# Four key tiles instead of five at both ends of a windowed attention, and the first two expert turns prepared one stage earlier

## What is computed

```python
def one_block(b):                       # b: one tile of 128 queries, 8 of them
    q0 = b * Q_BLOCK
    kb = lax.dynamic_slice_in_dim(k_pad, q0, span, axis=1)      # span = 128 + 2 * 128 keys, padded with zeros at both ends
    kpos = q0 + offs
    mask = (jnp.abs(qi[:, None] - offs[None, :]) <= WINDOW) & ((kpos >= 0) & (kpos < L))[None, :]
    return sink_attend(qb, (kb, k_ctx), (vb, v_ctx), (mask, None), sinks)
...
p = softmax(concatenate(parts + [sink], axis=-1))
...
xb = x_pad[rows]                        # experts: the rows of the tokens that chose expert e
hb = jax.nn.silu(xb @ w_gate[e]) * (xb @ w_up[e])
y.at[rows].add((hb @ w_down[e]) * wb[:, None])
```

## Time and profile before

| | |
|---|---|
| median of 3 runs | 2992.59 us |
| lowest and highest run | 2986.41 and 2995.37 us |
| the profiled execution | 2990.77 us, its span 2989.0 us |
| mean granted clock of TensorE | 0.979 of full speed |
| attention, first to last PE instruction | 259.8 to 556.7 us, granted clock 1.00 from 300 us on |
| mixing of layer 0, then its experts | 558.3 to 795.1 us, then from 797.3 us |
| experts of layer 1 | from 2050.4 us |

### The profile page before, as it was taken

How to read it: one execution, slowest core, us unless ns; L and a number is a source line. 1 busy time by engine, 2 the same in 40 slices (tenths; PEclk the granted TensorE clock), 3 DMA queues, 4 the chain that set the end, 5 groups by cost and what they waited for, 6 DMA issues and landing times. The chain is left out here.

```text
span 2989.0 us, 40809 instructions
## 1 busy us (share of the span) xinstructions
PE 2821.1 (94%) x15284; PEld 1368.5 (46%) x15287; DVE 1753.3 (59%) x3359; ACT 509.5 (17%) x1060; POOL 532.5 (18%) x404
## 2 busy tenths in 40 slices
PE   8998999999899999999999598997999999999994
PEld 3444666544444444444444264543444444444442
DVE  4994555466656555555555455665565555555555
ACT  1113555201110111111111240011110111111112
POOL 0000000111022222222222211101222222222212
PEclk9999999999999999999999899998999999999997
DMA  9777200201599999999999622017999999998996
GB/s 365 258 271 215 78 15 8 77 29 42 206 338 331 310 299 321 328 339 329 353 306 321 208 99 83 29 50 282 306 296 332 296 366 320 320 345 275 311 325 197
DMA packets 147086, 715.70 MB, mean 239 GB/s; under 512 B 16702, under 2 KB 21950, under 8 KB 94665
## 3 DMA queue, kind: packets, MB, share of 16 engines
q1 hardware_dynamic: 104252, 556.83, 48.6%
q0 software_dynamic: 42336, 154.16, 20.8%
q10 hardware_dynamic: 304, 2.11, 0.2%
HBM read 598.18 MB, written 114.84 MB: 239 GB/s over the span
## 5 line engine op out<-in xcount | busy, mean ns | idle before, releaser
L1668 PE MATMUL exG<-ring,xT 128*32 128x512 f32 (+2 forms) x2352 | 683.4, 596 | 5.2 <-DMA ring<-in_exp_w_up_dram 3.7
L1479 DVE COPY xT<-exX 128x512 f32<-128x512 f32 x146 | 101.0, 692 | 680.5 <-PE exX L1656 680.2
L1668 PEld LDWEIGHTS exG<-ring,xT 128*32 128x32 f32 (+2 forms) x2352 | 240.0, 141 | 348.0 <-issue 343.4
L1702 PE MATMUL exD<-ring,ex_hT 128*32 128x512 f32 (+2 forms) x1176 | 353.2, 603 | 1.7 <-DVE w_fnet L1517 0.8
L1612 ACT ACTIVATE ex_hT<-exH 128x256 f32<-128x256 f32 x144 | 55.2, 383 | 1454.5 <-PE exH L1690 1454.5
L1485 DVE RECIPROCAL ex_e<-ex_e 128x256 f32<-128x256 f32 x142 | 249.0, 1753 | 5.0
L1668 PE MATMUL exG<-oT,xT 128*32 128x512 f32 (+2 forms) x592 | 192.5, 597 | 1.3 <-DVE xT L1479 1.3
L1426 POOL DMA_INDIRECT y_scratch<-w_fnet,idx_out x72 | 136.1, 1891 | 299.1 <-DMA y_scratch<-w_fnet,idx_out 156.3
L1426 POOL DMA_INDIRECT y_scratch<-w_o,idx_out x72 | 132.8, 1844 | 306.3 <-DMA y_scratch<-w_o,idx_out 166.8
L1449 DVE TENSOR_TENSOR mod<-place,slots 128x1024 bf16<-128x1024 f32 (+3 forms) x196 | 174.1, 912 | 8.1 <-PEq L235 7.4
L1668 PE MATMUL exG<-w_fnet,xT 128*32 128x512 f32 (+2 forms) x608 | 172.2, 599 | 4.8 <-DMA ring<-in_exp_w_up_dram 4.8
(11 more groups left out here) (414 smaller groups left out, 4338.8 us busy)
## 6 DMA issues: line engine op xcount, KB each, us to landing
ring<-in_exp_w_gate_dram SPq DMA_DIRECT2D x64, 1024.0 KB
ring<-in_exp_w_up_dram SPq DMA_DIRECT2D x64, 1024.0 KB
ring<-in_exp_w_down_dram SPq DMA_DIRECT2D x64, 1024.0 KB
ada_w<-in_w_ada_dram SPq DMA_DIRECT2D x48, 512.0 KB, 5.6
oT<-in_exp_w_gate_dram SPq DMA_DIRECT2D x17, 1024.0 KB, 10.4
oT<-in_exp_w_up_dram SPq DMA_DIRECT2D x17, 1024.0 KB, 14.1
oT<-in_exp_w_down_dram SPq DMA_DIRECT2D x17, 1024.0 KB
fT<-in_exp_w_gate_dram SPq DMA_DIRECT2D x17, 1024.0 KB, 10.4
```

The lines of the kernel that those rows point to most:

```text
L1479: dve.tensor_copy(xT[:, par, 0:KT // 2], psX[:, 0:KT // 2]).then_inc(xT_d, 1)
L1668: last = pe.matmul(psG[par][p:p + m], xT[:, par, k, p:p + m], ring[s % RING][:, 0:2, k * FF:(k + 1) * FF], start=k == 0, stop=k == KT - 1)
L1702: last = pe.matmul(psD[p:p + m, c], hT[:, k * P + p:k * P + p + m], ring[s % RING][:, 2, k * D + c * 512:k * D + (c + 1) * 512], start=k = ...
```

## The change

The first and the last query tile no longer touch the key tile that lies outside the sequence: two near tiles and two context tiles, 512 columns for a head instead of 640. `near_tiles`, `width` and `halves_of` give the tiles, the columns and the two halves of a pair's buffer. The mask is now three 128-column tiles that all query tiles share, and its load comes ahead of the first load of the queries. In a pair of an end tile all context products wait on `near_mm`.

In the mixing stage the first two turns are prepared instead of one: both one-hot matrices, both sets of indices, both gathers; `down(7)` goes ahead of the index products. The split of the routing weights and the reading out of the first two turns' weights move into the experts' stage, the latter (`first_weights`) into the middle of the first `gate_up`. The indices of turn 3 are read out in the middle of the second `gate_up`.

```diff
-    none = np.full((P, P), gone)
-    mask = np.stack([np.stack([none if t == 0 else before, 0 * none, none if t == NT - 1 else after], 1) for t in range(NT)], 1)
+    mask = np.stack([before, 0 * before, after], 1)
...
+                def near_tiles(t):
+
+                    return range(max(0, t - 1), min(NT, t + 2))
+
+                def width(p):
+
+                    near = len(near_tiles(p // PAIRS)) * P
+                    return near, near + CTX
...
+                        sp.dma_start(mask[:].rearrange("p t s -> p (t s)").bitcast(mybir.dt.uint16), A["mask"]).then_inc(mask_in, 16)
                         load(0)
-                        sp.dma_start(mask[:].rearrange("p t s -> p (t s)").bitcast(mybir.dt.uint16), A["mask"]).then_inc(mask_in, 16)
...
+                            if len(tiles) < 3:
+                                pe.wait_ge(near_mm, p + 1)
+                                for j in range(2):
+                                    last = pe.matmul(sc[j][:, W:S], q[j], far[j], start=True, stop=True)
+                                last.then_inc(score_mm, 1)
+                                return
...
-                        pool.wait_ge(idx_done, 1)
-                        pool.indirect_dma_start(out=xg[:, 0], out_offset=None, in_=u_dram,
-                                                in_offset=bass.IndirectOffsetOnAxis(ap=idx[:, 0:1], axis=0)).then_inc(gathered[0], 16)
+                        pool.wait_ge(idx_done, 2)
+                        for b in range(2):
+                            pool.indirect_dma_start(out=xg[:, b], out_offset=None, in_=u_dram,
+                                                    in_offset=bass.IndirectOffsetOnAxis(ap=idx[:, b:b + 1], axis=0)).then_inc(gathered[b], 16)
...
+                        def weight_parts():
+                            link = Links(dve, parts_own)
+                            for c in range(3, 6):
+                                link(dve.tensor_copy(moving[:, :, :, c], w_rest))
+                                if c < 5:
+                                    link(dve.tensor_tensor(w_rest, w_rest, moving[:, :, :, c], ALU.subtract))
+
+                        def first_weights():
+                            dve.wait_ge(first_mm, 1)
+                            dve.tensor_reduce(w_all[:, 0:2], psD[:, :, 3:6], AX, ALU.add).then_inc(first_own, 1)
+                            dve.tensor_copy(idx_all[:, 0:2], idx[:])
...
-                        onehot(1, 1)
-                        indices(0, 0, 2)
+                        rows(0, 0, 2)
+                        weight_parts()
+                        first_weights()
                         onehot(2, 0)
-                        indices(1, 1, 2)
-                        rows(0, 0, 2)
+                        rows(1, 1, 2)
                         indices(2, 0, 2)
-
                         onehot(3, 1)
-                        rows(1, 1, 2)
+                        hidden(0, 0, 2)
                         indices(3, 1, 2)
-                        hidden(0, 0, 2)
...
                             for k in range(KT):
+                                if b == 0 and k == KT - 2:
+                                    first_weights()
+                                if b == 1 and k == KT // 2:
+                                    index(3, 1)
```

More of the change, by code:

```diff
@@ L698, in heads, with halves_of @@
                     return t, (2 * c + a) * 4 + 2 * half
-                def slot(t, j):
-                    return t + j if j < 3 else NT + 2 + j - 3
+                def near_tiles(t):
[3 more added lines that the diff above has]
+                    return near, near + CTX
+                def slot(t, j):
+                    near = near_tiles(t)
+                    return near[j] + 1 if j < len(near) else NT + 2 + j - len(near)
+                def halves_of(p, buf):
+                    s = width(p)[1]
+                    return [buf[:, j * s:(j + 1) * s] for j in range(2)]
                 with nc.Block() as block:
@@ L852, in scores @@
                             at_least(pe, copied_d, p - 1)
-                            sc = pair[p % 2]
+                            sc, tiles, (W, S) = halves_of(p, pair[p % 2]), near_tiles(t), width(p)
                             q = [qT[j * HD:(j + 1) * HD, t % 2, k] for j in range(2)]
-                            near = [kT[j * HD:(j + 1) * HD, kv, t * P:t * P + W] for j in range(2)]
+                            near = [kT[j * HD:(j + 1) * HD, kv, slot(t, 0) * P:slot(t, 0) * P + W] for j in range(2)]
@@ L856, in scores @@
                             far = [kT[j * HD:(j + 1) * HD, kv, (NT + 2) * P:(NT + 2) * P + CTX] for j in range(2)]
                             for j in range(2):
-                                last = pe.matmul(sc[:, j * S:j * S + W], identb[:], mask[:, t], start=True, stop=False)
+                                pe.matmul(sc[j][:, 0:W], identb[:], mask[:, slot(t, 0) - t:slot(t, 0) - t + len(tiles)], start=True, stop=False)
                             for j in range(2):
-                                last = pe.matmul(sc[:, j * S:j * S + W], q[j], near[j], start=False, stop=True)
+                                last = pe.matmul(sc[j][:, 0:W], q[j], near[j], start=False, stop=True)
@@ L913, in mix @@
         def mix(layer, src, w, logits, place, moving, ids, skey, slots, small,
[L914 removed]
+                hot, pad, idx, xg, own_sems, yo_out, w_rest, load_in, load_down, expert):
             with ExitStack() as ctx:
@@ L1427, in add @@
                                                     in_=yo[:, par], in_offset=None, compute_op=ALU.add).then_inc(added, 16)
-                        for b in range(1, 4):
+                        for b in range(2, 4):
                             gather(b, b % 2, 2)
@@ L1657, in turn_rows, with first_weights @@
                             last.then_inc(X_mm, 1)
+                        def first_weights():
+                            pe.wait_ge(parts_own, 5)
+                            for b in range(2):
+                                for t in range(NT):
+                                    for _, r, p, m in pieces(turns[b]):
+                                        last = pe.matmul(psD[p:p + m, b, 0:6], hot[:, b, t, p:p + m], moving[:, t, r, :],
+                                                         start=t == 0, stop=t == NT - 1)
+                            last.then_inc(first_mm, 1)
                         def gate_up(b, par):
```

117 lines of the change are left out of this document (65 added, 52 removed).

## The result

The changed kernel takes 2999.28 us (median of 20 runs, 2993.78 to 3006.07), the kernel before 2995.59 us (20 runs on the same chip); the ratio is 1.0013, 95% interval 1.0007 to 1.0019. The prediction said 11 us faster; it is 4 us slower: 0.13%, but the interval lies clear of 1. The profiled execution took 2994.38 us with a span of 2992.6, 3.6 more than the one before.

What follows compares the result with a forecast made beforehand. PE, busy 94% of the span, was taken as the bound. Attention 8.0, end of mixing 0, experts of layer 0 -0.5 and of layer 1 3.5 sum to 11.0 us gained: 2981.6 us, range 2975 to 2988.

Steps and rivals of the forecast that it cites:

- the end of mixing: Mixing to experts: POOL's second gather replaces SP as the last to finish; stage shortens by -0.1 to +0.8 us, taken as 0.
- Layer 0: Start of layer 0's experts: result 0, at most +1.5 us, with a possible clock drop costing about 1.8; taken as -0.5.
- The wait for the third gather: Layer 0's experts, before turn 2's transposes: PE waits 2.5 us for the rows of turn 2.
- Its landing: Layer 0's experts: turn 2's gather lands near 821.5, based on an earlier gather that took 9.1 us under load.
- The issue: Layer 0's experts: turn 2's gather is issued at 812.7 instead of 803.56, its indices being ready later.
- That fall: Layer 0's experts: if 2.5 us of idleness drop PE's clock, about 1.8 us is lost.
- Layer 1: Start of layer 1's experts: weights 3.1 us earlier, minus 0.5 for index 3, plus 0.9 for the clock: gain 3.5.
- Attention: Attention stage: 2.0 us at the start, 5.4 from the narrower pairs, 0.6 at the last pair; gain 8.0.
- the clock is down in other places than now: Whole kernel: one of three conditions under which the prediction called itself wrong; no size given.
- the 2.0 forecast: Start of attention: smaller mask goes first, so the queries release PE at about 257.8 instead of 259.78; gain 2.0 us.
- The 6.0 forecast for the pairs and their end: Attention's 16 narrower pairs: 0.31 us for each of eight, 0.37 for the others, together 5.4, plus 0.6 at the last pair.
- Rival (d): End tiles of attention: PE's clock falls, so the kernel gets slower; all 16 pairs would cost over 40 us; chance 0.03.

Runs made afterwards that it cites:

- e3: Changed kernel with the second gather issued at the start of the experts' stage instead of in mixing; 1.0012 of the kernel before, 2995.23 us.
- e7: Changed kernel with SyncE's weight loads reordered, the first expert's down weights no longer loaded in mixing; 0.9998 of the kernel before, 2995.40 us.
- e4: Changed kernel with both gathers issued at the start of the experts' stage, none in mixing; 0.9997 of the kernel before, 2992.85 us.
- e2: Kernel before with only the preparation part of the change (mixing, experts and their caller); 1.0027 of the kernel before, 3000.70 us.
- e9: Kernel before with its one mixing gather issued at the start of the experts' stage instead; 1.0025 of the kernel before, 3001.70 us.
- e1: Kernel before with only the attention part of the change; 0.9987 of the kernel before, 2988.22 us.
- e6: Changed kernel with no gather in mixing and turn 2's indices prepared earlier; 0.9973 of the kernel before, 2987.41 us.

## Why the prediction was wrong

**The step that failed** is the end of mixing: "POOL ends at 794.2 to 795.2 ... So POOL takes the place of SP, and the stage shortens by -0.1 to +0.8. I take 0." It read the end of a gather from the row of its issue. POOL's rows ended even a little before the forecast (788.6, which is 793.8 in the time of before, as `place` is 5.2 us earlier). But the stage doesn't end with the issue; it ends when the gathers' packets are through (four openings in the two traces; e3 and e7 move the one with the other, and e4 takes the wait away). They stand behind 3 MB of weights and the last store, now with 1 MB instead of 0.5: issued at 786.14, the first gather has no packet before 790. The stages grew by 3.2 and 3.4 us (2.3 and 3.1 in e2). The kernel before had the same wait, and its cost was 1.3 us, since `down(7)` covered the rest (e9). By putting `down(7)` ahead of the index products the change made everything but the gathers earlier. That cover was never priced.

**Layer 0** was to lose 0.5 and loses 5.2 from the opening on (`gate_up(2)` 34.4 us after it instead of 29.2), and 2.9 in the trace of e2, where the same code stands. The wait for the third gather was named with 2.5 and came as 4.0 (4.2 in e2). Its landing was put too early: 10.6 us after the issue instead of 8.8, and 10.8 in e2. The issue came 16.3 us after the opening instead of 15.4, but 15.0 in e2, so that term was right but for the clock: six of the eight pieces of `gate_up(0)` took 8.3 us in after and 6.9 in e2. And the clock fell after the wait, 0.9 on the transposes and 1.9 on `down(0)` (0.1 and 1.5 in e2). That fall was in the text with 1.8 and was given too little weight. The formula of the Trainium skill ("DMA: Bandwidth & Descriptors", "Anatomy of one DMA"), 2.0 us plus bytes over 436 GB/s, stays far off: 10.6 us under load. The same page puts most of its fixed time behind the last byte; the 1.3 to 1.7 us from the last packet to the opening fit that.

**Layer 1** was to gain 3.5. From the opening on `gate_up(1)` gains 2.1 and `gate_up(2)` 2.6, the low end of the forecast, for the clock fell there too. With 3.4 lost at the opening, it loses 0.8.

**Attention** was to be 8.0. In the trace of after each part was right to 0.1 us (start, drain, maximum, both periods), and e1 shows 7.9. What failed is "the clock is down in other places than now" as a mere proviso. The four traces with the old attention have the clock back (their first half microsecond wholly at 2.4 GHz) 3.5 to 4.7 us after the first product, and A between 304.2 and 304.4. The eight with the narrow tiles and no extra products have it back after 7.4 to 19.5 us, and A between 296.4 and 302.2, a mean gain of 5.1. Two terms make up that spread. The start: the queries release PE 3.7 to 3.9 us after the opening in five of the eight, but 5.3 to 5.5 after it in e3, e4 and e6, so that of the 2.0 forecast only 0.2 to 0.4 is left there; why they land later in these isn't known. And the clock: from the first product on, 292.7 to 293.0 us pass where it is back after 7.4 to 8.2 us, 294.5 to 294.7 where it takes 13.4 to 13.6, and 296.8 to 296.9 where it takes 19.5, against 298.5 to 298.6 with the old attention. The 6.0 forecast for the pairs and their end is 5.9 at best and 1.7 at worst. That e1 came out at 7.9 was the lucky end of both. Rival (d) had the mechanism, the clock in the end tiles, but looked for it in all 16 pairs; it happens in the first few.

**The sum.** Attention 5.1 in the mean and the preparation -7.8 by e2 give -2.7; measured is -3.7. In the two profiled executions attention gives 6.0, M0 -8.4 and M1 -0.8, together -3.2; the difference is 3.6. What remains goes both ways: 0.7 before attention starts, and in layer 0 a wait of 2.3 us at 921 dropped the clock before (0.62 from 921 to 925), while one of 2.5 us at 924 dropped nothing after, which cost the kernel before 1.5. Near 2250 after loses 2.1: PE waits 5.36 us for the up weights of one expert there, before it waited 3.69, and the clock falls. The same wait is 3.0 to 3.9 in the traces of before and eleven experiments, with either preparation, and 4.8 in e6; it looks like chance of single executions.

## What to carry to other kernels

In this kernel a stage that ends with a gather doesn't end at its issue: look for the last packet of the gather's queue, and for what stands ahead of it. Before moving work in front of a late transfer, ask what it was hidden behind; here `down(7)` was that cover, and the remedy was to issue the gathers after the barrier, their indices being ready, and to load less ahead of them. And a transfer that is made early pays only if the next in the chain doesn't become late; here the third gather took back what the first two gave.

## What was unexpected of the hardware

TensorE's clock at the start of attention stayed at 1.2 GHz for 7.4 to 19.5 us with PE busy 3.93 of 4 us in one window, and in the kernel before, less busy, for 3.5 to 4.7. Four products that nothing reads, ahead of the first scores, brought the clock back 3.3 and 3.9 us after the opening in the two traces that have them. Why the narrow tiles do this is open: no run changed the pairs' rhythm alone. One candidate stands in the rows and is untested: in each narrow pair PE stands still for 0.07 us between the near and the context products (260.33 to 260.40 in after), where the kernel before has context products that don't wait. The Trainium skill ("TensorE: Matmul & The Clock Gate", "Part 1: The HAM clock gate") says that the number of slow products at a start varies from run to run of one kernel; the eight traces, of which the attention part is the same, agree.
